# The last pair's old-state output of each head group turned back inside the next unit of main products

## Chip, cores and metric

One core of one Trainium2 chip. The metric is device time in microseconds, the median of several executions; lower is better.

## The reference, cut to what matters

One layer of a hybrid decoder on 256 prompt tokens and 64 sample tokens (8 sequences of 8), all in float32. The part that the change touches is the state space mixer, in 8 groups of 8 heads:

```python
proj = n1 @ w_in                       # z, x/B/C, dt, short convolution, gates
xbc_c = silu(causal_dwconv(xbc, xbc0)) # per group: B, C and four tiles of x
y_off = einsum('bclgn,bcgrpn,bclgr->bclgrp', Cm, h_prev, exp(Acum))
y = (y_diag + y_off + D * xs) * silu(z)
yg = y * rsqrt(mean(y * y over the group) + EPS)   # one norm per group
branch_a = (yg * ssm_norm) @ w_ssm_out
```

`y_off` is what the old states give: for the prompt the state after the first chunk, for each sample sequence its own state `state_ssm`. A layer goes on with a gated short convolution, a merge, a ConvFFN and a gated embedding.

## The kernel before

All products hold tokens in the free dimension (320 columns) and channels on the partitions. A weight arrives as a *piece* of 512 KB (128 rows x 1024), by the SP queue into a ring of 4 buffers `raw`. ACT makes its upper part `whi` (`split_hi`, line 679), VectorE the lower part `wlo` (line 1029), and TensorE multiplies three times a tile: `n_hi x whi`, `n_lo x whi`, `n_hi x wlo` (`three`, lines 1614 to 1616). A *unit* (line 1693) is 2 pieces, 128 output channels, 48 products; its halves are the pieces. Splits are made 3 pieces ahead: while the unit with pieces n and n+1 is at work, ACT and VectorE split pieces n+3 and n+4, ahead of their other work for that unit. The SP queue loads pieces in twos: the load of pieces n and n+1 waits until piece n-3 is wholly split (`lo_split`, line 597).

The order on each engine is written out by hand as steps (lines 91 to 103). For a group after the first, the steps are: units x0 (B), x1 (C), the norm of the group before, x2, x3, `bc`, x4, eight `out` pieces of the group before, x5, z0, `ssd1`, z1, `ssd3`, pair 0, z2, `last`, pair 1, z3, pair 2, pair 3. Then the next group's x0. Groups 1 to 7 are a loop; group 0 and the short convolution's first round (which begins with the unit `c0` and a norm step) stand outside.

In a *pair* (two heads) TensorE makes the diagonal part (line 1982), the old-state output of the prompt (1993) and of the samples (1997), the new states (`carry_in`, 1831), and, for the first three, turns the next pair's states (`turn_states`). The samples' output comes out with tokens on the partitions; ACT copies it to `yo` (942, `yo_kept`), and TensorE turns it back into columns 256 to 383 of the same PSUM bank (2006, `yoff_done`). VectorE waits for that, then weighs and adds (1297 to 1301) and tells `yg_ready`. ACT waits for `yg_ready` before its square (948), then stores the new states, and goes on in its order. Pair 3 uses PSUM bank 1, which the next group's x1 writes; x1 waits for `yg_ready` of the whole group (line 1639).

Behind x0, ACT issues two loads of the next states, 512 KB each (`load_pair`, 692), then copies x0 out of PSUM (891, 892) for VectorE's convolution (1150 to 1155). The SP queue issues, behind the load of piece 6, the group's decay tables (lines 577 to 588, 1 MB and three smaller ones). The norm step is: a product with ones (2010), `var` and a reciprocal on VectorE (1304, 1306), a square root on ACT (958), four products and four lower parts (1310, 1313). On VectorE and ACT it stands ahead of the splits of pieces 7 and 8.

Of the kernel before, what the change touches and what calls it, by code (L numbers as in the profile page):

```python
# [155 lines left out]
def hybrid_decoder(nc, ins, outs, scratch):  # L156
# [7 lines left out]
    with ctx:  # L164
# [1444 lines left out]
        def _(pe):  # L1609
# [8 lines left out]
            def piece_ready(seg, it, pos):  # L1618
                wait(pe, lo_split, first_piece(seg, it) + pos + 1)
                return (seg.piece0 + pos) % RING  # L1620
# [5 lines left out]
            def bank_free(seg, it, step):  # L1626
# [61 lines left out]
                if kind == "pg":  # L1688
                    pe.wait_ge(ple_kept, 3)
                    pe.wait_ge(sigs, 32 + 4 * it + j - 3)  # L1690
                    return j

            def unit(seg, it, step, pos):
                bank = bank_free(seg, it, step)
                for half in range(2):
                    slot = piece_ready(seg, it, pos + half)
                    for kk in range(8):
                        k = 8 * half + kk
                        last = three(ps[:, bank, 0:NT], tiles(whi[slot], kk), tiles(wlo[slot], kk),
                                     n_hi[:, k, :], n_lo[:, k, :], k == 0, k == KM - 1)  # L1700
                    last.then_inc(multiplied, 1)
# [132 lines left out]
            def tasks(seg, it, step, pos):  # L1834
# [75 lines left out]
                elif kind == "dturn":  # L1910
                    pe.wait_ge(dt_done, 1)
                    for bank, i in ((2, 0), (3, 1)):
                        for c in range(3):
                            rows = P if c < 2 else NS
                            last = turn(ps[0:rows, bank, c * HEADS:(c + 1) * HEADS], wm[0:HEADS, i, token_rows(c)],
                                        ident[0:HEADS, 0:HEADS])
                    last.then_inc(dt_turned, 1)
                elif kind == "dtab":
                    pe.wait_ge(consts_ready, N_CONSTS)
                    pe.wait_ge(a_kept, 1)  # L1920

                    def dta(c, rows):
                        return wm[0:rows, 4, c * HEADS:(c + 1) * HEADS]
                    for bank, inner, inner_s in ((4, tri[:], tri_s[:, 0:NS]), (5, after[:], after_s[:])):
                        for c in range(2):
                            mm(ps[:, bank, c * HEADS:(c + 1) * HEADS], inner, dta(c, P), start=True, stop=True)
                        last = mm(ps[0:NS, bank, 2 * HEADS:3 * HEADS], inner_s, dta(2, NS), start=True, stop=True)
                    last.then_inc(dt_sums, 1)
                    for c in range(2):
                        mm(ps[0:HEADS, 7, c * P:(c + 1) * P], dta(c, P), tri[:], start=True, stop=True)  # L1930
                    mm(ps[0:HEADS, 7, SEQ:NT + NB], dta(2, NS), tri_s[:], start=True, stop=True).then_inc(row_sums, 1)
                elif kind == "bc":
                    pe.wait_ge(xs_ready, 6 * g + 2)
                    wait(pe, yg_ready, 4 * g)
                    if seg.start == 0:
                        pe.wait_ge(heads_ready, 1)
                    for c in range(3):
                        rows = P if c < 2 else NS
                        last = turn(ps[0:rows, 5, c * P:(c + 1) * P], bc[:, 0, token_rows(c)], ident[:])
                    last.then_inc(bt_done, 1)  # L1940
                    for c in range(3):
                        rows = P if c < 2 else NS
                        last = mm(ps[0:rows, 6, c * P:c * P + rows], bc[:, 0, token_rows(c)], bc[:, 1, token_rows(c)],
                                  start=True, stop=True)
                    last.then_inc(cb_done, 1)
                elif kind == "ssd1":
                    pe.wait_ge(xs_ready, 6 * g + 6)
                    wait(pe, vsum_read, g)
                    if seg.start == 0:
                        pe.wait_ge(rows_kept, 2)  # L1950
                    wait(pe, out_added, 8 * g)
                    for c in range(3):
                        rows = P if c < 2 else NS
                        for q in range(4):
                            last = turn(ps[0:rows, 2 + c, q * P:(q + 1) * P], xs[:, q, token_rows(c)], ident[:])  # L1955
                        last.then_inc(xt_done, 1)
                elif kind == "ssd3":
                    pe.wait_ge(xw_ready, 2 * g + 2)
                    pe.wait_ge(b_stacked, 2 * g + 2)
                    mm(ps[:, 2, :], bt[:, 0, :], xwe[:, 0, :], start=True, stop=True).then_inc(h1_done, 1)  # L1960
                    turn_states(g, 0)
                elif kind == "last":
                    pe.wait_ge(hn_added, 8 * g + 2)
                    for q in range(4):
                        last = turn(ps[:, HN_BANKS[0], q * P:(q + 1) * P], h1t[:, q * P:(q + 1) * P], ident[:])
                    last.then_inc(last_done, 1)
                    for q in range(4):
                        last = mm(ps[:, HN_BANKS[1], q * P:(q + 1) * P], xwe[:, 1, q * P:(q + 1) * P], bt[:, 1, :],
                                  start=True, stop=True)
                    last.then_inc(last_done, 1)  # L1970
                elif kind == "pair":
                    pe.wait_ge(w_ready, 5 * g + 5)
                    pe.wait_ge(cbm_ready, g + 1)
                    if j:
                        pe.wait_ge(hn_added, 8 * g + 2 * j - 1)
                    for c in range(3):
                        rows = P if c < 2 else NS
                        for i in range(2):
                            h = 2 * j + i
                            quad_i = 2 * c + h // 4 if c < 2 else 4  # L1980
                            m = h % 4 if c < 2 else h
                            last = mm(ps[i * HD:(i + 1) * HD, 6, token_rows(c)],  # L1982
                                      xdt[0:rows, c, h * HD:(h + 1) * HD], wm[0:rows, quad_i, m * rows:(m + 1) * rows],
                                      start=True, stop=True)
                    last.then_inc(yd_done, 1)
                    pe.wait_ge(h1_kept, g + 1)
                    pe.wait_ge(t_kept, 8 * g + 2 * j + 2)
                    if j in (1, 2):
                        pe.wait_ge(yg_ready, 4 * g + j)
                    if j == 3:  # L1990
                        pe.wait_ge(z_ready, 4 * g + 4)
                    bank = YOFF_BANKS[j]
                    mm(ps[:, bank, 0:P], h1t[:, j * P:(j + 1) * P], bc[:, 1, token_rows(1)], start=True, stop=True)  # L1993

                    for half in range(2):
                        for b in range(4):
                            last = mm(ps[b * NS // 2:(b + 1) * NS // 2, bank, P:2 * P],  # L1997
                                      c_own_mem[:, half * P + b * NS // 2:half * P + (b + 1) * NS // 2],
                                      h0t[:, 4 * half + b, :], start=half == 0, stop=half == 1)
                    last.then_inc(yo_done, 1)  # L2000
                    pe.wait_ge(x_stacked, 2 * g + 2)
                    carry_in(g, j)
                    if j < 3:
                        turn_states(g, j + 1)
                    pe.wait_ge(yo_kept, 4 * g + j + 1)
                    turn(ps[:, bank, 2 * P:3 * P], yo[:], ident[:]).then_inc(yoff_done, 1)
                elif kind == "norm":
                    pe.wait_ge(ysum_ready, 3 * g)
                    pe.wait_ge(hn_added, 8 * g)
                    mm(ps[:, VS_BANK, 0:NT], ones[:], zs[:, 0, :], start=True, stop=True).then_inc(vs_done, 1)  # L2010
                elif kind == "rows":
                    turn_rows(it)
                elif kind == "end":
                    pe.wait_ge(y_gained, 3 * (KM // 4 - 1))
                    turn_rows(KM // 4, range(3))
                    pe.wait_ge(sq_added, ADDED[4] + 8)
                    last_sums(sq_sum, True)
                    turn_rows(KM // 4, range(3, 4))
                    pe.wait_ge(sq_ready, SQUARES[4] + 8)
                    last_sums(sq_pair[1], False).then_inc(sq_summed, 1)  # L2020
# [40 lines left out]
```

## Time and profile before

| | us |
|---|---|
| median of 3 runs | 2895.76 (2895.06 to 2896.71) |
| the profiled execution | 2895.49 |
| its span, first to last instruction | 2893.8 |
| TensorE busy in it | 2849.4 (98%) |
| weight loads of TensorE busy | 2794.8 (97%) |
| VectorE, ACT, GpSimd busy | 1748.3, 1200.0, 288.7 |
| mean granted clock of TensorE | 0.995 |

The kernel keeps TensorE at work nearly throughout; the clock is full almost everywhere. Busy time of TensorE is modelled, so what counts is the distance from one product's start to the next, and idle time in front of a product. Idle time of the other engines tells how much later their work could come. The eight ends of groups lie at 148, 266, 385, 504, 622, 741, 860 and 978 us.

### The profile page before, as it was taken

The numbers are of one execution on the slowest core, as the hardware profiler recorded it, in microseconds if no ns is written. First come the engines' busy times: TensorE is split into PE (matmuls) and PEld (weight loads), VectorE is DVE, ScalarE is ACT, GpSimd is POOL, SyncE is SP. The second block draws the span as 40 slices with busy tenths as digits, with TensorE's granted clock in tenths as the row PEclk, the third lists the DMA queues.
The fourth block names the chain that finished last, engine by engine and source line by source line (L and its number), as shares of the span: only waits on it lengthen the run. The fifth ranks groups of instructions, "written<-read, shape, count | busy, mean of one in ns | idle before, by whom it ended". The sixth has DMA issues, their size and how long they took to land.

```text
span 2893.8 us, 52916 instructions
## 1 busy us (share of the span) xinstructions
PE 2849.4 (98%) x19824; PEld 2794.8 (97%) x19824; DVE 1748.3 (60%) x2228; ACT 1200.0 (41%) x1792; POOL 288.7 (10%) x456
## 2 busy tenths in 40 slices
PE   7999999999999999999999999999999999999998
PEld 6899999999999899999999999999999999999998
DVE  7676876777768655455455555655555555555564
ACT  4554544545445433333333334433333333333543
POOL 2221222111212100000000001000000000000100
PEclk9999999999999999999999999999999999999999
DMA  7566565665656665555555555554455555545463
GB/s 204 155 187 184 147 200 156 183 182 153 200 150 180 186 158 148 146 150 154 145 147 154 151 145 148 145 154 145 145 158 146 145 148 154 147 145 156 134 177 109
DMA packets 753280, 457.33 MB, mean 158 GB/s; under 512 B 14633, under 2 KB 747233, under 8 KB 752625
## 3 DMA queue, kind: packets, MB, share of 16 engines
q1 hardware_dynamic: 679433, 414.21, 50.3%
q10 hardware_dynamic: 73096, 39.39, 4.7%
q0 software_dynamic: 672, 2.66, 0.2%
q8 instruction: 52, 0.85, 0.1%
q14 instruction: 27, 0.22, 0.0%
HBM read 430.73 MB, written 25.47 MB: 158 GB/s over the span
## 4 chain that ended last, share of the span: by engine, by line
PE 95%; DVE 2%; issue 1%; ACT 1%; DMA 0%; POOL 0%; ACTq 0%; SPq 0%; DVEq 0%; POOLq 0%
PE ps L1614 29%; PE ps L1615 29%; PE ps L1616 29%; PE ps L1821 1%; PE ps L1982 1%; PE ps L1831 1%; PE ps L1997 1%; PE ps L1993 0%; PE ps L1848 0%; DVE wlo L1029 0%; PE ps L1726 0%; PE ps L1955 0%; PE ps L1736 0%; PE ps L1727 0%; DVE nt L1061 0%
## 5 line engine op out<-in xcount | busy, mean ns | idle before, releaser
L1614 PE MATMUL ps<-n_hi,whi 128*128 128x320 f32 x4144 | 1288.6, 311 | 5.5 <-issue 4.5
L1616 PE MATMUL ps<-n_hi,wlo 128*128 128x320 f32 x4144 | 1282.1, 309 | 0.0
L1615 PE MATMUL ps<-n_lo,whi 128*128 128x320 f32 x4144 | 1282.1, 309 | 0.0
L1029 DVE TENSOR_TENSOR wlo<-raw,whi 128x1024 fp32r<-128x1024 f32 x746 | 923.7, 1249 | 495.4 <-ACT whi L679 494.4
L679 ACT ACTIVATE whi<-raw 128x1024 fp32r<-128x1024 f32 x746 | 783.8, 1057 | 860.6 <-PE ps L1616 790.7
L1614 PEld LDWEIGHTS ps<-n_hi,whi 128*128 128x128 f32 x4144 | 779.5, 188 | 9.2 <-issue 6.5
L1615 PEld LDWEIGHTS ps<-n_lo,whi 128*128 128x128 f32 x4144 | 779.6, 188 | 0.6
L1616 PEld LDWEIGHTS ps<-n_hi,wlo 128*128 128x128 f32 x4144 | 779.3, 188 | 0.0
L1614 PE MATMUL ps<-c_hi,whi 128*128 128x320 f32 x1728 | 534.8, 309 | 2.0 <-issue 1.5
L1615 PE MATMUL ps<-c_lo,whi 128*128 128x320 f32 x1728 | 534.0, 309 | 0.0
L1616 PE MATMUL ps<-c_hi,wlo 128*128 128x320 f32 x1728 | 534.0, 309 | 0.0
L1614 PEld LDWEIGHTS ps<-c_hi,whi 128*128 128x128 f32 x1728 | 324.3, 188 | 2.7 <-issue 1.8
L1615 PEld LDWEIGHTS ps<-c_lo,whi 128*128 128x128 f32 x1728 | 324.4, 188 | 0.0
L1616 PEld LDWEIGHTS ps<-c_hi,wlo 128*128 128x128 f32 x1728 | 324.3, 188 | 0.0
L1325 DVE TENSOR_TENSOR xt<-xt,ps 128x640 f32<-128x640 f32 x120 | 98.5, 821 | 149.2 <-PE ps L1616 149.2
L796 ACT ACTIVATE c_hi<-chunk 128x320 fp32r<-128x320 f32 x76 | 35.9, 472 | 192.1 <-DVE chunk L1388 83.5
L1489 POOL COPY ftail<-spad 128x18 f32 (+1 forms) x44 | 10.3, 234 | 860.5 <-ACT spad L986 860.5
L1546 POOL TENSOR_TENSOR hn<-h,ea 128x512 f32<-128x512 f32 x64 | 71.6, 1143 | 232.3 <-DMA out_ssm_sample<-hn 232.3
L1325 DVE TENSOR_TENSOR acc_a<-acc_a,ps 128x640 f32<-128x640 f32 x64 | 52.5, 821 | 42.3 <-PE ps L1616 42.0
L1150 DVE TENSOR_SCALAR scv<-spad,scol 128x336 f32<-128x336 f32 x44 | 20.3, 460 | 86.2 <-ACT spad L986 86.2
L1153 DVE SCALAR_TENSOR_TENSOR cv<-xpad,gcol,cv 128x344 f32<-128x344 f32 x96 | 67.2, 700 | 3.4
L1489 POOL COPY xtail<-xpad 128x27 f32 (+1 forms) x48 | 27.7, 578 | 393.3 <-ACT xpad L892 393.1
(295 smaller groups left out, 1808.3 us busy)
## 6 DMA issues: line engine op xcount, KB each, us to landing
raw<-in_w_in SPq DMA_DIRECT2D x322, 512.0 KB, 5.1
raw<-in_w_ffn_gate SPq DMA_DIRECT2D x88, 512.0 KB, 4.3
raw<-in_w_ffn_up SPq DMA_DIRECT2D x88, 512.0 KB, 5.0
raw<-in_w_ffn_down SPq DMA_DIRECT2D x88, 512.0 KB, 4.1
raw<-in_w_ssm_out SPq DMA_DIRECT2D x64, 512.0 KB, 4.3
h<-in_state_ssm ACTq DMA_DIRECT2D x32, 512.0 KB, 5.6
out_ssm_sample<-hn ACTq DMA_DIRECT2D x32, 512.0 KB, 4.4
raw<-in_w_sc_out SPq DMA_DIRECT2D x32, 512.0 KB, 4.0
```

Of the source, the lines that this page charges most:

```text
L679: activate(whi[slot][:], raw[slot][:], copy).then_inc(hi_split, 1)
L796: activate(c_hi[:, j, :], chunk[:, j, :], copy).then_inc(c_hi_ready, 1)
L1029: tt(wlo[slot][:], raw[slot][:], whi[slot][:].bitcast(F32), SUB).then_inc(lo_split, 1)
L1153: own(stt(dst, pad[:, k:k + n], weights[k], dst, MUL, ADD))
L1325: tt(dst, dst, ps[:, b0:b0 + 2, 0:NT], ADD).then_inc(out_added, 1)
L1489: g_.tensor_copy(tail[:, :, :, at(t)].rearrange("p i k a -> p i (k a)"), last_rows(pad, taps)).then_inc(kept, 1)
L1546: g_.tensor_tensor(hn[j % 2][:, b, :], h0[j % 2][:, b, :], ea[:, j, P + NS + 4 * half:P + NS + 4 * half + 4].unsqueeze(2) .broadcast_to([P ...
L1614: mm(out, w_h, x_h, start=first, stop=False)
L1615: mm(out, w_h, x_l, start=False, stop=False)
L1616: return mm(out, w_l, x_h, start=False, stop=last)
L1821: last = turn(ps[:, 4 + half, b * P:(b + 1) * P], h0[j % 2][:, 4 * half + b, :], ident[:])
L1831: mm(ps[:, HN_BANKS[half], :], x_stack[:, half, j * P:(j + 1) * P], b_stack[:, half].rearrange("p b n -> p (b n)"), start=True, stop=True) ...
```

## The change

The last pair's turn (`turn_old(g, 3)`) is no longer issued at the end of pair 3. It is issued between the two halves of the unit that follows: x0 of the next group in the loop (`seg.start` is 1 there), and `c0` of the short convolution behind group 7. The wait for `yo_kept` goes with it. Pairs 0 to 2 stay as they were, and no other engine's program is changed.

```diff
--- before.py
+++ after.py
@@ -1690,9 +1690,18 @@
                     pe.wait_ge(sigs, 32 + 4 * it + j - 3)
                     return j
 
+            def turn_old(g, j):
+
+                pe.wait_ge(yo_kept, 4 * g + j + 1)
+                turn(ps[:, YOFF_BANKS[j], 2 * P:3 * P], yo[:], ident[:]).then_inc(yoff_done, 1)
+
             def unit(seg, it, step, pos):
                 bank = bank_free(seg, it, step)
                 for half in range(2):
+                    if half and seg.name == "ssm" and seg.start and step[1:] == ("x", 0):
+                        turn_old(it - 1, 3)
+                    if half and seg.name == "sc" and seg.start == 0 and step[1:] == ("c", 0):
+                        turn_old(GROUPS - 1, 3)
                     slot = piece_ready(seg, it, pos + half)
                     for kk in range(8):
                         k = 8 * half + kk
@@ -2002,8 +2011,8 @@
                     carry_in(g, j)
                     if j < 3:
                         turn_states(g, j + 1)
-                    pe.wait_ge(yo_kept, 4 * g + j + 1)
-                    turn(ps[:, bank, 2 * P:3 * P], yo[:], ident[:]).then_inc(yoff_done, 1)
+                    if j < 3:
+                        turn_old(g, j)
                 elif kind == "norm":
                     pe.wait_ge(ysum_ready, 3 * g)
                     pe.wait_ge(hn_added, 8 * g)
```

## Rows read from the trace of the kernel before

**Rows 1.** the page's part 4, the chain that ended last, by engine
```profile
PE 95%; DVE 2%; issue 1%; ACT 1%; DMA 0%; POOL 0%; ACTq 0%; SPq 0%; DVEq 0%; POOLq 0%
```

**Rows 2.** waits of weight loads (PEld), whole span: total us, times, longest
```profile
PEld ps L2006 <- ACT yo L942: 3.3, 8, 0.4
```

**Rows 3.** timeline of weight loads at that end: start, us, line, [idle before <-releaser]
```profile
621.92 0.30 PEld L1831 LDWEIGHTS ps<-b_stack,x_stack 96*128 96x128 f32 x2 [0.20 <-issue]
622.63 0.14 PEld L2006 LDWEIGHTS ps<-ident,yo 128*128 128x128 f32 x1 [0.42 <-ACT yo L942]
623.29 0.19 PEld L1614 LDWEIGHTS ps<-n_hi,whi 128*128 128x128 f32 x1 [0.52 <-issue]
```

**Rows 4.** timeline of TensorE (PE), a turn ahead of a z unit
```profile
597.48 0.27 PE L2006 MATMUL ps<-ident,yo 128*128 128x128 f32 x1
...
597.74 0.30 PE L1615 MATMUL ps<-n_lo,whi 128*128 128x320 f32 x1
```

**Rows 5.** timeline of ACT behind the end at 622 us
```profile
625.16 0.47 ACT L948 ACTIVATE zs<-chunk 128x320 f32<-128x320 f32 x1 [2.58 <-DVE chunk L1301]
...
630.92 1.04 ACTq L692 DMA_DIRECT2D h<-in_state_ssm  x2
...
634.16 1.06 ACT L679 ACTIVATE whi<-raw 128x1024 fp32r<-128x1024 f32 x1 [0.70 <-PE ps L1616]
637.68 0.39 ACT L891 ACTIVATE xpad<-ps 128x256 f32<-128x256 f32 x1 [2.46 <-PE ps L1616]
...
646.00 2.00 ACT L679 ACTIVATE whi<-raw 128x1024 fp32r<-128x1024 f32 x2
```

**Rows 6.** timeline of VectorE (DVE), the same stretch
```profile
623.67 0.28 DVE L1297 TENSOR_TENSOR yoffs<-ps,ea 128x128 f32<-128x128 f32 x1
...
624.63 0.49 DVE L1301 TENSOR_TENSOR chunk<-chunk,zs 128x320 f32<-128x320 f32 x1
627.30 2.36 DVE L1029 TENSOR_TENSOR wlo<-raw,whi 128x1024 fp32r<-128x1024 f32 x2 [2.17 <-ACT whi L679]
...
638.22 0.46 DVE L1150 TENSOR_SCALAR cv<-xpad,gcol 128x344 f32<-128x344 f32 x1 [0.87 <-ACT xpad L892]
...
647.11 2.36 DVE L1029 TENSOR_TENSOR wlo<-raw,whi 128x1024 fp32r<-128x1024 f32 x2
```

**Rows 7.** timeline of the SP queue: the load of piece 6
```profile
628.90 0.37 SPq L598 DMA_DIRECT2D raw<-in_w_in  x1
```

**Rows 8.** DMA issues, 628.5 to 629.4 us: KB each, us to landing
```profile
raw<-in_w_in SPq DMA_DIRECT2D x1, 512.0 KB, 4.0
```

**Rows 9.** DMA issues, 611.2 to 611.8 us: a state load with nothing ahead
```profile
h<-in_state_ssm ACTq DMA_DIRECT2D x1, 512.0 KB, 4.5
```

**Rows 10.** DMA rate while one queue streams, 615.5 to 616 us
```profile
DMA packets 343, 0.18 MB, mean 350 GB/s; under 512 B 1, under 2 KB 343, under 8 KB 343
```

**Rows 11.** DMA, 631 to 634.5 us: packets, MB, share (q1 SP, q10 ACT); issues
```profile
q1 hardware_dynamic: 922, 1.23, 102.7%
...
h<-in_state_ssm ACTq DMA_DIRECT2D x2, 512.0 KB, 11.3
```

**Rows 12.** DMA, 636 to 642 us, the same two queues
```profile
q1 hardware_dynamic: 1605, 0.94, 60.0%
q10 hardware_dynamic: 1674, 0.85, 55.7%
```

**Rows 13.** timeline of TensorE behind the norm's products
```profile
637.78 0.55 PE L1614 MATMUL ps<-n_hi,whi 128*128 128x320 f32 x1
```

**Rows 14.** timeline of TensorE behind the last group's end
```profile
982.94 0.48 PE L1614 MATMUL ps<-n_hi,whi 128*128 128x320 f32 x1 [2.38 <-issue]
...
1013.67 0.39 PE L1614 MATMUL ps<-c_hi,whi 128*128 128x320 f32 x1 [1.54 <-issue]
```

**Rows 15.** busy us of each engine by stretch, then granted clock, DMA share, GB/s
```profile
982.90:986.60 3.70, 3.66 (x14) 3.66 (x15) 1.23 (x1) 0.08 (x1) 0.13 (x2) 0.54 0.55 163
```

**Rows 16.** timeline of VectorE behind the last group's end
```profile
991.04 0.49 DVE L1304 TENSOR_SCALAR var<-ps 128x320 f32<-128x320 f32 x1 [1.67 <-PE ps L2010]
```

## The prediction

> **What bounds the kernel now.** I read the chain that ended last first: TensorE is 95% of it [rows 1], so a change counts only where it moves TensorE. Then the waits of TensorE's weight loads, where one belongs to the line that is moved: the turn waits for ACT's copy of `yo` 8 times, 3.3 us in all, 0.42 in the group that I follow [rows 2, 3]. Then the timelines of all queues from the end of one group to piece 7 of the next. Eight waits for eight groups, so one a group, at the last pair; I work on the end at 622 us, in the loop. The reader should see two things there. TensorE is not stopped by any other engine in what follows. But ACT, VectorE and the loads run a chain beside it whose end is nearly as late.
>
> **What the edit gives.** Weight loads: second `carry_in` product dispatched at 621.92 + 0.11 = 622.03, turn 622.63, next unit 623.29 [rows 3]. From the turn to the unit pass 0.66 us, mostly the loop's branch, which TensorE's sequencer reaches only after the wait. Without turn and wait I give the same 0.66 us from the second `carry_in` dispatch: the unit starts at about 622.70, 0.6 us sooner. Against it stands the turn inside the stream: in the one that already stands between transposes and a unit, 0.26 us pass from the turn to the unit's second product where 0.15 is the pitch [rows 4], so 0.1 us; going in and out of a unit may double it. I take 0.2 (bounds 0.1 and 0.3). TensorE is then 0.4 us ahead from the end of the unit on. With nothing else, 8 x 0.4 = 3.2 us, 0.1%.
>
> **What is queued behind the turn.** The turn now follows 24 products, one piece. A piece takes 3.52 us (ACT's releases at 634.16 and 637.68 are one apart [rows 5]), with 0.1 us for a first product and 0.1 for the switch: 622.70 + 3.72 = 626.4. VectorE can start `yoffs` 0.3 us behind that, at 626.7, instead of 623.67; its four operations end 1.45 us after the first began (624.63 + 0.49 [rows 6]), so `yg_ready` comes at 628.15 instead of 625.12, and ACT's square at 628.2 instead of 625.16 [rows 5]: 3.05 us later. Behind that wait stand, on ACT in order: the store of `hn`, the upper split of pieces 3 and 4, then the two state loads. On VectorE: the lower splits of 3 and 4. On the SP queue: the load of piece 6, which waits for the lower split of piece 3, and behind it the decay tables and pieces 7 to 9. On GpSimd: the last sum of squares and the small copies, which have microseconds of room before the norm.
>
> Two covers hold. Unit x1 needs `yg_ready` for its bank at about 622.70 + 7.3 = 630.0, and has it at 628.15. Pieces 3 and 4 are split by 632.7 (now two splits of 1.18 us from 627.30 to 629.66 [rows 6], and 3.05 later; the first by 631.6), and piece 3 is wanted at about 633.5.
>
> The third fails. The load of piece 6 is issued at 628.90 now and lands 4.0 us later, at 632.9 [rows 7, 8], well before ACT wants it at 634.16, when the slot is free [rows 5]. After the change it is issued at 628.90 + 3.05 = 631.95. The state loads, 2 of 512 KB, go out when x0 is done: 630.92 now, so 630.5 with TensorE 0.4 ahead; ACT's splits are dispatched by then. The order turns round: 1 MB goes ahead of piece 6. A state load alone lands 4.5 us after issue [rows 9], at 635.0; at 350 GB/s [rows 10] each further 512 KB takes 1.5 us, so the second state load lands at 636.5 and piece 6 at 638.0.
> That the later one stands at the back is what the kernel shows now: the state loads, issued at 630.92 behind piece 6 and the 1 MB table, need 11.3 us, and in 631 to 634.5 all the traffic is SP's queue, 102.7% of the engines, none of ACT's [rows 11]. Once both flow they share evenly [rows 12]. So the bounds are: alone, 631.95 + 4.0 = 636.0; even shares from the first packet, about 636.8; strictly behind, 638.0. I take 638.0, because the row on who gets the engines while an older transfer is being served is [rows 11].
>
> The Trainium skill says in "DMA: Bandwidth & Descriptors", section "Queues, rings and completion order", that each DMA engine goes round between the queues that have work, a packet at a time. By that rule the landing would be the middle bound. [rows 12] agree with it and [rows 11] do not.
>
> **What that costs.** ACT takes its work in order: piece 6's upper split 638.0 to 639.1, only then x1's copy out of PSUM (637.68 now [rows 5]). VectorE: lower split of 6 until 640.35, and only then the convolution of x1, which starts at 638.22 now [rows 6]. It is 2.1 us late. From there VectorE runs without slack through the convolution, the reciprocal and the gated norm to the lower split of piece 7, which ends at 647.11 + 1.22 = 648.33 [rows 6] and would end at 650.4; ACT's part of it is the split from 646.00. TensorE wants piece 7 at: first product behind the norm's, 637.78 [rows 13], plus 0.24 and three pieces of 3.52, 648.58. Its slack is 0.25 us. So TensorE, 0.4 ahead, waits some 2.2 us before piece 7 and goes on 2.1 - 0.25 = 1.85 us later than now. Later work is released by TensorE or by this same chain and shifts with it; nothing gives the loss back. The loads of pieces 7 to 9 start 3.05 later but have 3 us before ACT gets to them on the delayed chain.
> This stands at the heads of groups 1 to 7: 7 x 1.85 = 12.95 us.
>
> The last end goes to the short convolution. There TensorE stops after some 8 products for 2.38 us with no releaser, and runs 3.7 us at 0.54 of full clock, nearly the 1.2 GHz level [rows 14, 15], so the piece ends at 986.7 and the turn's results at about 988.6. By the distances above ACT splits 3 and 4 until about 991.3, VectorE until 992.9, and only then comes the norm's `var`, at 991.04 now [rows 16]: 1.85 us late. It feeds the 2.6 MB reload of `xt` and the loads behind it, which end in the idle 1.54 us of TensorE before 1013.67 [rows 14]. So 1.85 us once more.
>
> Sum: 12.95 + 1.85 = 14.8 us. The profiled execution is 2895.49 us (span 2893.8 and 1.7 around it), 0.27 under the median of 2895.76. Against the median I predict 2910.6 us.
>
> **The rivals.**
> - Even shares of the DMA engines. Piece 6 lands at 636.8, VectorE is 0.9 late, TensorE 0.65 a group: 7 x 0.65 + 1.85 = 6.4, 2902 us. For it [rows 12], against it [rows 11].
> - No contention that counts, piece 6 at 636.0 or sooner: its lower split ends at 638.3, where x1's convolution starts now; TensorE stays between -0.4 and 0 a group, and the last end gives 0 to 1.85: 2893 to 2898. Against it: 1 MB must fit in beside it. This is also the case in which the edit does what it says.
> - TensorE's clock. The idle 2.38 us was followed by 3.7 us at 0.54 [rows 14, 15]: 3.7 x 0.46 = 1.7 us lost. If each new stop of 2.2 us brings that too, add 7 x 1.7 = 12: 2922 us. Against it: that stop came behind the small products of the pairs, these would come behind dense ones.
> - Faster (the other side). The loop's branch hides wholly, the turn costs 0.1, the state loads do not delay piece 6, and in the last end the turn and its wait no longer stand ahead of the 2.38 us stop, so that the slow clock behind it goes: 7 x 0.5 + 1.7 + 0.6 = 5.8 us, 2890. It decides from the landing of piece 6: at most 635.6, which is 3.65 us after an issue at 631.95, less than the 4.0 alone.
>
> **How the numbers follow.** Forecast (2905 to 2916) 0.52; even shares (2898 to 2905) 0.18; clock (2916 to 2930) 0.12; no contention (2893 to 2898) 0.14; faster 0.04. What a measurement of this kernel can tell from no change is 0.2%, 5.8 us, so 2890.0 to 2901.6. Faster by more 0.04; within it, the third case and some of the second, 0.20; slower 0.76. The range 2897 to 2922 leaves out the faster case, most of the third and the upper half of the clock's, some 0.2.
>
> **What would show it.** In the changed kernel's timeline: the first product of x0 0.6 us behind the second `carry_in` weight load, no idle time ahead of it (right for the gain); the turn 3.7 us into the unit; ACT's square 3 us later; the state loads issued ahead of piece 6's load, and that landing over 5 us after issue; ACT waiting for that load, not for TensorE, before its sixth split; VectorE's x1 convolution with no idle time before it; and among TensorE's waits seven of 1.5 to 2.5 us on `wlo`. If the landing stays at 4 us, or TensorE shows no wait at piece 7, the sum is wrong; so it is if 648.58 hides a slack that the 0.15 us pitch does not show.

## The result, and the profile after

The kernel after takes 2916.11 us (median of 6 runs, 2910.3 to 2923.2), the kernel before 2894.68 us (median of 6 beside it, 2893.1 to 2896.7). The ratio is 1.0075, with an interval of 1.0064 to 1.0086: 21.4 us slower. The time lies inside the range and 5.5 us above the 2910.6 forecast. The profiled execution of after is 2916.39 us, with a span of 2914.7 (before: 2893.8), so the two traces differ by 20.9 us, nearly as much as the medians. One execution of the first experiment's kernel took 13071 us; it is left out of that kernel's median below.

I read the same views in the same order. First the chain that ended last, by engine, which was 95% TensorE before [rows 1]:

```profile
PE 88%; DVE 5%; DMA 2%; ACT 1%; issue 1%; POOL 0%; ACTq 0%; SPq 0%; DVEq 0%; POOLq 0%
PE ps L1614 27%; PE ps L1615 27%; PE ps L1616 27%; DMA raw<-in_w_in 2%; DVE wlo L1029 1%; PE ps L1830 1%; PE ps L1991 1%; ACT whi L679 1%; PE ps L1840 1%; PE ps L2006 1%; DVE var L1306 1%; PE ps L2002 0%; DVE cv L1153 0%; PE ps L1857 0%; DMA raw<-in_w_ssm_out 0%
```

A load of weights, `raw<-in_w_in`, now has 2% of it, and VectorE 5%. Then TensorE's waits over the whole span; among those of its weight loads the wait on `yo` of [rows 2] is gone:

```profile
PE ps L1614 <- DVE wlo L1029: 19.1, 8, 4.2
...
PE ps L1614 <- DVE acc_a L1325: 3.1, 1, 3.1
```

Now the loop. Groups are numbered 0 to 7 as in the code, group 0 ahead of the loop; the end at 622 us is where group 4 ends and group 5 begins. The second `carry_in` product there, which starts at 622.26 in before, starts at 635.53 here; all distances below count from it. TensorE and its weight loads (start, us, line, instruction, [idle before <-releaser]), the lines that answer to [rows 3, 4]:

```profile
635.19 0.30 PEld L1840 LDWEIGHTS ps<-b_stack,x_stack 96*128 96x128 f32 x2 [0.20 <-issue]
635.53 0.19 PEld L1614 LDWEIGHTS ps<-n_hi,whi 128*128 128x128 f32 x1
...
639.14 0.31 PE L1616 MATMUL ps<-n_hi,wlo 128*128 128x320 f32 x1
639.29 0.27 PE L1696 MATMUL ps<-ident,yo 128*128 128x128 f32 x1
639.31 0.39 PE L1614 MATMUL ps<-n_hi,whi 128*128 128x320 f32 x1
639.54 0.30 PE L1615 MATMUL ps<-n_lo,whi 128*128 128x320 f32 x1
...
660.89 0.31 PE L1616 MATMUL ps<-n_hi,wlo 128*128 128x320 f32 x1
663.29 0.42 PE L1614 MATMUL ps<-n_hi,whi 128*128 128x320 f32 x1 [2.09 <-DVE wlo L1029]
```

Nothing stands between `carry_in` and the unit, the turn goes by in the stream, and at piece 7 TensorE stops for the lower split. ACT, its queue, and SP's queue (answering to [rows 5, 7]):

```profile
641.10 0.47 ACT L948 ACTIVATE zs<-chunk 128x320 f32<-128x320 f32 x1 [5.24 <-DVE chunk L1301]
...
643.39 1.04 ACTq L692 DMA_DIRECT2D h<-in_state_ssm  x2
...
644.84 0.37 SPq L598 DMA_DIRECT2D raw<-in_w_in  x1
...
650.90 1.06 ACT L679 ACTIVATE whi<-raw 128x1024 fp32r<-128x1024 f32 x1 [4.97 <-DMA raw<-in_w_in]
...
660.90 1.99 ACT L679 ACTIVATE whi<-raw 128x1024 fp32r<-128x1024 f32 x2
```

The order has turned round: two state loads at 643.39 and 643.98, then piece 6 at 644.84, where piece 6 was 2.0 us ahead before. ACT stands idle 4.97 us for it; before it was TensorE that ACT waited for at this place [rows 5]. VectorE (answering to [rows 6]):

```profile
640.57 0.49 DVE L1301 TENSOR_TENSOR chunk<-chunk,zs 128x320 f32<-128x320 f32 x1
...
651.99 1.23 DVE L1029 TENSOR_TENSOR wlo<-raw,whi 128x1024 fp32r<-128x1024 f32 x1 [3.05 <-ACT whi L679]
653.13 0.46 DVE L1150 TENSOR_SCALAR cv<-xpad,gcol 128x344 f32<-128x344 f32 x1
...
662.02 2.35 DVE L1029 TENSOR_TENSOR wlo<-raw,whi 128x1024 fp32r<-128x1024 f32 x2
```

The convolution of x1 has no idle time ahead of it any more, and from its start to the lower splits with piece 7 pass 8.89 us, as before (638.22 to 647.11 in [rows 6]). What the DMA engines did in 645 to 647.5 us, and then in 648 to 650.7 us (packets, MB, share of the engines):

```profile
q10 hardware_dynamic: 1489, 0.75, 104.8%
...
raw<-in_w_in SPq DMA_DIRECT2D x1, 512.0 KB, 6.0
```

```profile
q1 hardware_dynamic: 1125, 0.88, 101.6%
q10 hardware_dynamic: 199, 0.09, 11.8%
```

From 645 to 647.5 all packets belong to ACT's queue and none to SP's, although piece 6's load had been issued at 644.84. SP's queue gets the engines only when the second state load is nearly through. It is [rows 11] with the parts changed, and the load takes 6.0 us instead of 4.0 [rows 8]: counted packet by packet, its first one comes 3.1 to 3.3 us after issue in all seven groups, where it is 1.0 to 1.1 in before.

By group, with each group's stop of TensorE ahead of piece 7 (from the product before it to the next, less the pitch of 0.15), the landing of piece 6 counted from the second `carry_in` product, and the group's length less that in before (from one end to the next; group 5 is the one followed above):

```
group              1      2      3      4      5      6      7
piece 6 lands    16.25  15.56  15.14  17.38  15.27  15.38  16.21   (before 10.7 to 11.1)
stop, us          3.22   2.52   2.13   4.38   2.25   2.34   3.20
half clock after  yes    no     yes    yes    yes    no     yes
group longer by   4.33   1.70   2.91   5.19   3.08   1.65   4.01   sum 22.9
```

The half clock is in the granted clock behind the stop (busy us by engine, then granted clock, DMA share, GB/s). The first line is group 5, from 1.6 us behind the end of its stop, the second the same place in group 6:

```profile
664.90:668.00 3.10, 3.10 (x13) 3.10 (x13) 2.74 (x4) 2.21 (x5) 0.54 (x2) 0.50 0.91 310
786.70:789.80 3.10, 3.10 (x25) 2.97 (x23) 2.81 (x4) 2.25 (x5) 0.60 (x2) 1.00 0.98 326
```

13 products against 25 in the same 3.10 us: TensorE ran at 1.2 GHz in one and at 2.4 GHz in the other. Each such stretch has some 12 products at 0.27 us instead of 0.15, 1.44 us lost. It begins 0.3 to 1.5 us behind the end of the stop.

Last, the end of group 7, which goes to the short convolution (answering to [rows 14 to 16]), TensorE, VectorE, and the granted clock behind the stop:

```profile
1003.30 0.31 PE L1614 MATMUL ps<-n_hi,whi 128*128 128x320 f32 x1 [1.29 <-issue]
...
1034.02 0.60 PE L1614 MATMUL ps<-c_hi,whi 128*128 128x320 f32 x1 [3.07 <-DVE acc_a L1325]
...
1005.80 0.29 DVE L1297 TENSOR_TENSOR yoffs<-ps,ea 128x128 f32<-128x128 f32 x1 [4.02 <-PE ps L1696]
...
1011.41 0.48 DVE L1304 TENSOR_SCALAR var<-ps 128x320 f32<-128x320 f32 x1
...
1001.50:1005.50 4.00, 2.71 (x20) 2.59 (x19) 0.28 (x1) 0.00 (x0) 0.00 (x0) 1.00 0.27 79
```

The stop there is 1.29 us instead of 2.38, and the clock stays at full. From group 7's `carry_in` to the end of the span it is 1914.36 us against 1915.47 before. The difference of the traces is then whole: 22.9 for the seven groups, -1.1 for the rest behind them, and -0.85 because the end of group 0 came that much sooner, 20.9 us. That last part stands ahead of the first moved turn, so the edit has no hand in it: in the traces of the ten kernels this end lies anywhere from 146.4 to 149.3.

### The profile page after: what moved, and what is told of

It reads as the page before. It is cut to its first block, busy times and chain, and to the rows that moved or that the text cites. A ratio compares the mean times of both kernels' runs of the same rounds, so it can differ in the third digit from the quotient of the medians.

```text
span 2914.7 us, 52923 instructions
## 1 busy us (share of the span) xinstructions
PE 2854.1 (98%) x19824; PEld 2801.7 (96%) x19824; DVE 1748.5 (60%) x2228; ACT 1199.5 (41%) x1792; POOL 292.7 (10%) x456
## 4 chain that ended last, share of the span: by engine, by line
PE 88%; DVE 5%; DMA 2%; ACT 1%; issue 1%; POOL 0%; ACTq 0%; SPq 0%; DVEq 0%; POOLq 0%
PE ps L1614 27%; PE ps L1615 27%; PE ps L1616 27%; DMA raw<-in_w_in 2%; DVE wlo L1029 1%; PE ps L1830 1%; PE ps L1991 1%; ACT whi L679 1%; PE ps L1840 1%; PE ps L2006 1%; DVE var L1306 1%; PE ps L2002 0%; DVE cv L1153 0%; PE ps L1857 0%; DMA raw<-in_w_ssm_out 0%
## 5 line engine op out<-in xcount | busy, mean ns | idle before, releaser
L1614 PE MATMUL ps<-n_hi,whi 128*128 128x320 f32 x4144 | 1291.6, 312 | 21.0 <-DVE wlo L1029 19.1
```

Of the source, the lines that this page charges most:

```text
L1614: mm(out, w_h, x_h, start=first, stop=False)
```

## The experiments

Four theories stood: A, the forecast's (piece 6's load stands strictly behind the state loads); B, the later `yg_ready` as such, through ACT's and VectorE's queues, with no part of the DMA; C, the turn's own cost inside TensorE's stream; later D, a loss in proportion to how late the turn comes. "Landed" and the like count again from the second `carry_in` product.

**The order of the loads.** In the kernel after, the two state loads are moved behind x1's copy out of PSUM. The turn, and with it piece 6's load, stays as late as in after.

```
-                    if j == 0:
-                        load_pair(g, 0)
-                        load_pair(g, 1)
 ...
+                    if j == 1:
+                        load_pair(g, 0)
+                        load_pair(g, 1)
                     if j:
                         silu_x(g, j - 1)
```

> The changed kernel with one edit on ACT: the two loads of the next states are issued behind x1's copy out of PSUM instead of behind x0's, so that nothing stands ahead of piece 6's load. Times are counted from the start of the last carry_in product. Theory A (the queue of transfers: piece 6 stands behind 1 MB of states, and its late landing is what costs): piece 6 is still issued at 9.3 us but lands 4.1 us later, at 13.4, instead of at 15.1 to 17.4; x1's convolution starts at about 15.7 (15.96 before the change, 17.5 to 19.7 behind it); no wait of TensorE on wlo at piece 7 over 0.5 us, no half clock in the loop; 2889 to 2893 us, that is 23 to 27 below the changed kernel. Theory B (the late turn costs by itself, since ACT's square, the splits of pieces 3 and 4 and the order on VectorE are 2.7 us late whatever the transfers do): the stops before piece 7 stay above 1.5 us and the time above 2908. Theory C (the transpose inside the stream of products, or the stop of the clock that it brings, costs by itself): 2905 or more, half clock stays.

Measured: 2895.01 us, ratio 1.000 (0.9992 to 1.0009); the kernel before took 2894.81 beside it. All but 0.2 of the 21.4 us are gone, though the turn and `yg_ready` are where after has them. SP's queue and ACT in group 5 (its `carry_in` at 622.81), then TensorE's waits:

```profile
632.12 0.37 SPq L598 DMA_DIRECT2D raw<-in_w_in  x1
...
636.71 1.06 ACT L679 ACTIVATE whi<-raw 128x1024 fp32r<-128x1024 f32 x1 [3.95 <-DMA raw<-in_w_in]
637.60 0.41 ACTq L692 DMA_DIRECT2D h<-in_state_ssm  x1
...
PE ps L1614 <- DVE wlo L1029: 3.2, 6, 1.0
```

Piece 6 is issued at the same 9.31 as in after and has its first packet 1.0 us after issue, not 3.2, and lands after 3.9 to 4.9 us, not 5.8 to 8.1. What stops remain are at most 1.2 us and no group shows half clock. What B and C foretold, 2905 and more, did not come. It is 2 us over the 2889 to 2893 expected: a load with nothing ahead took up to 4.9 us, not 4.1, and landed at 13.3 to 14.2, late enough to use up the lead.

The same move in the kernel before is the control, since it could have had a worth of its own.

> Control: the kernel before, with the state loads behind x1's copy as in e1. Theory A (piece 6's place in the queue of transfers): piece 6 is already ahead of the states there and lands at 10.8 us behind the last carry_in product, with time to spare, so nothing changes: 2893 to 2897 us. If the gain of e1 came from moving the state loads as such, this would gain too: some 20 us, or as much as x1's convolution starts sooner.

Measured: 2895.21 us, ratio 1.000 (0.9991 to 1.0010), as expected. Moving the state loads is worth nothing where piece 6 is ahead of them; it gains only where piece 6 is behind them.

**Piece 6 early, turn late.** The other way round: the turn stays at 24 products, and SP's load of piece 6 waits for the split of piece 2, whose buffer it takes, not of piece 3.

```
-                        wait(sp, lo_split, base + pos + 1 - RING + 1)
+                        own_slot = seg.name == "ssm" and seg.start and pos == 6
+                        wait(sp, lo_split, base + pos - RING + 1 + (0 if own_slot else 1))
                         sp.sem_inc(loads_let_go, 1)
+                    if seg.name == "ssm" and seg.start and pos == 7:
+                        wait(sp, lo_split, base + pos - RING + 1)
```

> The changed kernel with one edit on the SP queue, in the loop over groups: piece 6 waits only for the split of piece 2, whose buffer it takes, instead of for that of piece 3; piece 7 waits for piece 3. The late turn then no longer holds piece 6 back, and the state loads stay where the change put them. Theory A: piece 6 lands before x0 is half done, x1's convolution starts with x1's end, at about 15.2 us behind the last carry_in product; no stop at piece 7; TensorE keeps its whole lead of 0.8 us a group; 2886 to 2891 us. Theory B (late square and splits cost by themselves): stops over 1.5 us stay, over 2908. Theory C (the transpose in the stream): 2905 or more.

Measured: 2890.1 us, ratio 0.9985 (0.9976 to 0.9993). The load goes out 5.7 us ahead of group 4's end (`carry_in` at 618.66), as the third of these, and lands 0.9 behind it, where after issued it 9.3 us behind the end:

```profile
611.43 2.27 SPq L601 DMA_DIRECT2D raw<-in_w_in  x3
```

Each group takes 117.84 us, 0.84 less than before, and TensorE doesn't stop in the loop. The square still comes at 5.57 and the turn still stands behind 24 products, so with this run B and C fall wholly. And the edit does gain, in every group, once the load is out of its reach.

**A late load without the edit.** In the kernel before, piece 6's load is held until the first piece of x1 has been multiplied. The turn isn't touched.

```
+                    if seg.name == "ssm" and seg.start and pos == 6:
+                        wait(sp, multiplied, base + 3)
```

> The kernel before, turn at its old place, with piece 6's load alone held until x1's first piece is multiplied (11.9 us behind the last carry_in product), in the loop over groups. It is then issued behind the state loads, at about 12.3. Theory A: it lands at 16.4 or later, x1's convolution starts at 18.7 instead of 15.96, TensorE stops some 2.5 us before piece 7 in seven groups (17.5 us), and in several the clock falls to half behind the stop (some 1.4 us each): 2912 to 2925 us. Theories B and C: the turn is where it was, so nothing of size is lost: under 2900 us.

Measured: 2927.94 us, ratio 1.0115 (1.0100 to 1.0130), 3 us over what was expected. Group 5 (`carry_in` at 638.83): SP's queue, ACT, TensorE, granted clock, then all waits of the kind:

```profile
650.89 0.37 SPq L600 DMA_DIRECT2D raw<-in_w_in  x1
...
655.51 1.06 ACT L681 ACTIVATE whi<-raw 128x1024 fp32r<-128x1024 f32 x1 [5.47 <-DMA raw<-in_w_in]
...
667.90 0.64 PE L1616 MATMUL ps<-n_hi,whi 128*128 128x320 f32 x1 [2.60 <-DVE wlo L1031]
...
667.90:671.60 3.70, 3.70 (x15) 3.70 (x16) 3.59 (x6) 2.94 (x5) 2.00 (x4) 0.56 0.63 207
...
PE ps L1616 <- DVE wlo L1031: 19.7, 8, 3.7
```

The load lands at 15.7 to 17.6, much as in after, and the same waits come back: 19.7 us in 8, where after has 19.1 in 8. Half clock follows in all seven groups. A late load of piece 6, with what stands behind it on SP's queue, makes the loss without the edit. It is larger here because TensorE has no 0.8 us of lead to set against it, and the clock drops seven times, not five.

**Where the turn stands.** In after it follows 24 products of the unit. These three put it behind 6, 12 and 18.

```
                     for kk in range(8):
                         k = 8 * half + kk
+                        if k == 2 and seg.name == "ssm" and seg.start and step[1:] == ("x", 0):
+                            turn_old(it - 1, 3)
+                        if k == 2 and seg.name == "sc" and seg.start == 0 and step[1:] == ("c", 0):
+                            turn_old(GROUPS - 1, 3)
 ...
```

(k == 4 and k == 6 for 12 and 18 products; the two calls between the halves of the unit go.)

> The changed kernel with the turn 6 products into the next unit instead of 24: 0.9 us instead of 3.6. Theory A: yo is copied 0.3 us behind the last carry_in product, so TensorE does not wait; VectorE's own hn sums end at 1.5 us, so yg_ready is at 3.0 us as before the change; piece 6 is loaded at 6.7 us, ahead of the state loads, and lands by 11; no stop at piece 7; TensorE ahead by 0.8 us a group; 2886 to 2891 us. Theory B agrees here, since the turn is not late. Theory C (the transpose in the stream of products, wherever it stands): over 2900.

> The changed kernel with the turn 12 products into the unit (at 2.0 us behind the last carry_in product; 6 gave 2886.8 us, 24 give 2916). Theory A: ACT's square at 3.8, piece 6 issued at about 7.6, still ahead of the first state load at 7.86; it lands at about 12, x1's convolution starts with x1's end, no stop at piece 7: 2885 to 2890 us, though the turn is 1 us later than with 6. Theory D (each microsecond of lateness costs in proportion, 29 us for 18 products): 2896 us.

> The changed kernel with the turn 18 products into the unit (at 2.9 us). Theory A: piece 6 is issued at about 8.45, behind the first state load (7.86) and together with the second (8.45): it lands between 13.0 (one load ahead) and 14.6 (both), x1's convolution starts at 15.3 to 16.9, and TensorE stops for 0.3 to 1.9 us before piece 7: 2889 to 2905 us, most of the loss between 12 and 24 products falling where the order of issue turns round. Theory D (in proportion): 2906 us.

Measured: 2886.8 us (0.9974, 0.9963 to 0.9985), 2886.8 us (0.9973, 0.9962 to 0.9984), 2897.3 us (1.0010, 1.0001 to 1.0020); with after, 24 products give 2916.1. SP's load of piece 6 and ACT's two state loads, behind 12 products (`carry_in` at 620.70) and behind 18 (623.86), and TensorE's waits of the latter:

```profile
628.25 0.37 SPq L598 DMA_DIRECT2D raw<-in_w_in  x1
...
628.56 1.04 ACTq L692 DMA_DIRECT2D h<-in_state_ssm  x2
```

```profile
632.29 0.37 SPq L598 DMA_DIRECT2D raw<-in_w_in  x1
...
631.73 1.04 ACTq L692 DMA_DIRECT2D h<-in_state_ssm  x2
...
PE ps L1614 <- DVE wlo L1029: 7.2, 8, 1.4
```

Behind 12, piece 6 is 0.3 us ahead of the state loads and lands 4.0 to 4.5 after its issue; they land at 17.0 and 20.9 and nobody misses them. Behind 18, it is issued between the two, with the second state load 0.02 us behind it. The DMA queues of that kernel in 633 to 634.7 us, in 635.3 to 636, and in 636.3 to 637.3:

```profile
q10 hardware_dynamic: 686, 0.35, 70.8%
```

```profile
q1 hardware_dynamic: 451, 0.23, 108.7%
q10 hardware_dynamic: 26, 0.01, 5.6%
```

```profile
q1 hardware_dynamic: 320, 0.19, 60.4%
q10 hardware_dynamic: 324, 0.17, 54.7%
```

The state load that was issued ahead has the engines to itself, as in after. Then piece 6 has nearly all of them for some 1 us, and only then does the state load that was issued 0.02 us behind it share them evenly. Piece 6 lands at 14.1. Behind 24 products both state loads are ahead of it and both have the engines first. 6 products later cost nothing from 6 to 12, 10.5 us from 12 to 18, and 18.8 us from 18 to 24, the last with the clock drops in it. D, which asked for 2896 and 2906, falls.

The lateness of the load has a price of its own all the same. Groups 1 to 7 together take 824.9 us behind 12 products, 830.3 in the first experiment's kernel (turn late, nothing ahead of piece 6) and 853.5 in after. Of the 28.6 us between 12 and 24 products, 5.4 go with a load that is late but alone, 23.2 with the 1 MB ahead of it. The versions behind 6 and 12 products are 8 us under the kernel before and 29 under after.

**The clock's part.** To part stop and clock, the kernel after was given 14 products of `n_hi` with itself ahead of piece 7's wait; they fill the stop and no one reads them.

```
+                    if half and seg.name == "ssm" and seg.start and step[1:] == ("x", 3):
+                        for kk in range(14):
+                            mm(ps[:, 3, 0:NT], n_hi[:, kk, 0:P], n_hi[:, kk, :], start=True, stop=True)
                     slot = piece_ready(seg, it, pos + half)
```

> The changed kernel with 14 products more in each group of the loop, of n_hi with itself into a free PSUM bank whose result nobody reads, ahead of the wait for piece 7 (2.06 us of TensorE work at 0.147 us each, against stops of 2.1 to 4.4 us). Theory A with the clock as its second part: the stops shrink to 0.1 to 2.4 us, what they wait for comes as before, and the half clock behind them goes in at least the groups with short stops: 5 x 1.4 us less, 2907 to 2912 us. If the half clock does not come from TensorE's idle time, or the clock costs nothing: as the changed kernel, 2914 to 2918; if the 14 products are not hidden: up to 14 us above it.

Measured: 2937.88 us, ratio 1.0147 (1.0130 to 1.0164). It missed, by a cost that none of the theories had. The end of group 4 (`carry_in` at 646.20), TensorE and granted clock, and the waits:

```profile
649.85 0.63 PE L1614 MATMUL ps<-n_hi,whi 128*128 128x320 f32 x1 [3.25 <-issue]
...
650.30:654.50 4.20, 4.20 (x17) 4.20 (x17) 0.00 (x0) 0.00 (x0) 0.00 (x0) 0.50 0.02 4
...
PE ps L1614 <- issue: 19.6, 7, 3.3
...
PE ps L1614 <- DVE wlo L1029: 3.8, 5, 1.1
```

At the heads of groups 2 to 7 TensorE stops right behind `carry_in` for up to 3.3 us with no engine as releaser, and half clock follows each time. The only other difference is a longer loop body, and the queues' totals over the span, after's line first, show what it brings:

```profile
q8 instruction: 52, 0.85, 0.1%
```

```profile
q8 instruction: 106, 1.74, 0.3%
```

From 300 to 1000 us after has no packet on the queue that loads instructions; this kernel has 48, of 16 KB each. In each of the six stops one starts 0.25 to 0.36 us behind `carry_in` and takes 1.1 to 1.6 us, and TensorE goes on 1.6 to 1.8 us behind its end. The likely reading is that the longer body is loaded anew in every round and TensorE stops for it; which engine's instructions these are the trace doesn't say, and at what length this begins no run shows.

Only group 1 is clean of it. There the fill cut the stop from 3.22 to 1.07 us, TensorE went on at the same place to within 0.1 us, half clock did not follow, and the group took 121.11 us instead of 122.73, 1.62 less. That fits the clock's price in after, but it is one group of one trace.

## Why the prediction was right, and where its terms were off

**The gain.** Forecast was a unit 0.6 us sooner, 0.2 for the turn, 0.4 a group in all. Measured: x0's first product 0.23 us behind `carry_in`, where it was 1.04, so 0.8; and from there to the norm's first product (units x0 and x1) it is 14.19 us with the turn and 14.18 without, so the turn in the stream costs nothing that can be seen. The branch that was to keep 0.66 us is hidden. The kernels without a stop in the loop show the same size, 0.84 a group. The gain was twice the forecast.

**What is queued behind the turn.** The square comes at 5.57 instead of 2.90: 2.67 later, where 3.05 was forecast, since the turn came at 3.75 and TensorE started sooner. Piece 6's load was issued 2.67 later, at 9.31, behind both state loads. This step held, and the runs on the turn's place show that it carries the result.

**The landing.** Taken was strictly behind, 15.74 in these counts (638.0 less 622.26). The mean of the seven is 15.88, so [rows 11] was the right row to choose. That it is so near is partly chance: the second state load landed at 13.4 to 13.7 and not at 14.2 (636.5 less 622.26), and piece 6 1.7 to 4.0 us behind it and not 1.5. In 645 to 647.5 us, with a load of each queue issued, the trace shows 1489 packets of one queue and none of the other.

The Trainium skill's rule of "DMA: Bandwidth & Descriptors", section "Queues, rings and completion order", that the engines go round between queues with work packet by packet, would have given 14.5. The trace disagrees with it as the prediction used it, for loads issued before another queue's. Whether SP's queue had its packets ready in that time the trace doesn't show, so the alternation itself is not refuted. Behind 18 products the trace agrees with it from 636.3 us on (320 and 324 packets), not in the 0.7 us before (451 and 26).

What the forecast had not is the spread, 15.14 to 17.38: the load takes 5.8 to 8.1 us in the same code. It comes at its very end: of its 1024 packets the 900th starts at 14.10 to 14.34 in every group, the last at 14.66 to 16.88. Before, the last start at 10.12 to 10.68. Behind it on the same queue stands the 1 MB table with packets of 4 KB; whether those hold up single engines was not tried.

**What it costs.** Landing to convolution: forecast 2.35 us, measured 2.33. TensorE's own need of piece 7: forecast 25.92, measured 25.51, the difference being the larger lead. The stop: forecast 2.2 us, measured 2.13 to 4.38, mean 2.86. In the two groups that kept full clock the net is 1.70 and 1.65 against 1.85. Over seven, stops less a lead of 0.8 give 7 x 2.06 = 14.4 us where 12.95 stood.

**The clock, the term that was left out.** This rival had a chance of 0.12, on the ground that the stop would come behind dense products. It came true in five of seven groups: 5 x 1.44 = 7.2 us, more than the 5.5 by which the forecast was short. The groups' own lengths say rather more: length gained, less the stop, plus the lead of 0.8, is 1.6 us in four of the five and 1.9 in group 1, against 0.0 and 0.1 in the two at full clock. The ground against the rival was wrong: dense products ahead of a stop do not keep the clock. In the kernel before with piece 6 held, all seven stops, of 2.2 to 3.8 us, were followed by half clock; in the other runs none of the stops before piece 7, of up to 1.5 us, were. Between them the sizes do not decide: in after 2.34 and 2.52 kept full clock, 2.13 and 2.25 did not. What does is open.

**The last end.** Forecast +1.85, measured -1.1: this step failed. It took [rows 14, 15], the 2.38 us stop and the slow clock behind it, as fixed. With the turn and its wait gone from ahead of it the stop was 1.29 us and the clock stayed, so the piece ended 5.2 us behind `carry_in` and not 8.4, `yoffs` started at 5.50 and not at about 10, and `var` came at 11.11, 1.6 us earlier than before, not later. The traces show what moves with it: a 16 KB packet on the queue that loads instructions, which starts 2.22 us behind `carry_in` in before and 0.65 in after, and behind whose end TensorE goes on, at 4.65 and at 3.01. This was a part of the "faster" rival, and so was the hidden branch; both came about, but not the early landing on which that rival hung. Later, at 1030, TensorE pays back a part in a 3.07 us wait on `acc_a`, with half clock behind it. The size of this term is uncertain. In three kernels with the same instructions there (after, the one with the state loads later, and the one with piece 6 early) the stop was 1.29, 1.8 and 2.1 us. Behind the 2.1 half clock followed, and from `carry_in` to the end of the span that kernel took 1916.09 us, 0.6 more than before.

Together: 14.4 + 7.2 for the loop, 1.3 more (about 1.1 of it the clock's, by the groups' lengths above), -1.1 and -0.85 at the two ends, 20.9 us; forecast were 12.95 + 1.85. So the path was right, the clock's step was wrong, the last end's step was wrong, and it is luck that the sum comes within 5.5 us: what the loop costs more was in part made good by the last end (2.95 less than forecast) and by a start that came 0.85 sooner. The 2916.1 us stand at the border between the forecast's case, to 2916, and the clock's, from 2916.

## What to carry to other kernels

When an instruction is moved later, follow the semaphore that it feeds to every queue, and write down which DMA transfers go out behind it and which other loads they now stand behind. Here six products' delay cost nothing as long as one load kept its place, 10 us when one load came to stand ahead of it, and 19 more when both did and TensorE's clock fell. A small step that others wait for belongs as early in the new place as it is free: behind the first products, not in the middle of the unit.

## What the runs showed of the hardware

- Two queues do not always share. A 512 KB load issued 0.9 us behind the second of two of another queue had no packet until 3.1 to 3.3 us after its issue (1.0 when alone), while the other streamed at about 345 GB/s. A load issued 0.02 us ahead of another had nearly all packets first (451 to 26 in 0.7 us) and then shared evenly. That order of issue decides is my reading of these two and of [rows 11, 12]; no run was made for it alone.
- A stop of TensorE between dense products, of 2.1 to 4.4 us, was followed in 12 of 14 cases before piece 7 by some 12 products at half clock (1.44 us), once by 20; such a stop therefore cost up to 1.7 times its length.
- 14 more matmuls in a loop's body brought a stop of up to 3.3 us at the head of each round that no engine released, with a 16 KB packet of instructions in it; without them the loop ran from 300 to 1000 us with no such packet.
